# Expert weights in 2 MB transfers, a ring of eleven double slots, and first loads inside the output projection

## What is computed

```python
# x1: the input plus the gated output of the mixer, y_conv and y_ssd (1024 x 1024 each)
x  = x + g1 * (concat([y_conv, y_ssd]) @ w_out)            # w_out 2048 x 2048
h  = modulate(rms_norm(x, norm2_w), sh2, sc2)
s  = sigmoid(h @ w_router)                                 # 32 experts in 8 groups of 4
best = argmax over groups of (sum of the top 2 of s + bias)
idx, gw = top 2 experts inside that group; gw normalised
y  = sum over the two experts e of gw * ((silu(h @ w_gate[e]) * (h @ w_up[e])) @ w_down[e])
out = rms_norm(x + g2 * y, final_norm_w)
```

## Time and profile before

| | |
|---|---|
| median of 3 runs | 2704.45 us |
| the profiled execution | 2700.38 us |
| its span | 2698.6 us |
| TensorE matmul, busy share | 94% |
| VectorE, ScalarE, GpSimd, busy share | 49%, 24%, 11% |
| moved by DMA | 710.43 MB, mean 263 GB/s |
| weights of the experts | 128 + 128 transfers of 1 MB, 64 of 2 MB, each some 31 us from issue to landing |

### The profile page before, as it was taken

One profiled execution on the slowest core, in us unless ns is written; L12 is line 12 of the kernel. 1 busy time (PEld: TensorE's weight loads), 2 busy tenths in 40 slices (PEclk: granted clock), 3 DMA queues, 4 the chain that ended last, 5 costly groups with the idle time before them and its releaser, 6 DMA issues.

```text
span 2698.6 us, 31563 instructions
## 1 busy us (share of the span) xinstructions
PE 2526.9 (94%) x11968; PEld 1517.0 (56%) x11968; DVE 1317.0 (49%) x1583; ACT 641.1 (24%) x897; POOL 295.4 (11%) x505
## 2 busy tenths in 40 slices
PE   4999999999999978999999699899999999999996
PEld 3577888888768866788887333233333333333332
DVE  4369999999785768544336522122222212121224
ACT  4122222222222286322333011011111111011113
POOL 0000000000021111010001111111111111111110
PEclk9999999999999989999999799999999999999998
DMA  9843333333586562755645999999993999999698
GB/s 336 309 130 101 101 109 101 98 109 97 152 287 209 190 218 90 285 170 153 227 132 210 421 414 409 405 362 415 406 407 114 392 403 370 408 406 408 224 412 340
DMA packets 234071, 710.43 MB, mean 263 GB/s; under 512 B 26292, under 2 KB 120644, under 8 KB 186382
## 3 DMA queue, kind: packets, MB, share of 16 engines
q1 hardware_dynamic: 186626, 555.56, 53.4%
q0 software_dynamic: 37344, 125.76, 14.9%
q10 hardware_dynamic: 9998, 27.71, 2.8%
HBM read 657.60 MB, written 69.81 MB: 270 GB/s over the span
## 4 chain that ended last, share of the span: by engine, by line
PE 33%; DMA 23%; DVE 2%; issue 0%; ACT 0%; SPq 0%; POOL 0%; ACTq 0%; DVEq 0%; POOLq 0%
DMA ring<-in_w_down_dram 19%; PE ps L1750 12%; PE ps L1764 7%; PE ps L1979 4%; PE ps L1981 4%; PE ps L1980 4%; DMA ring<-in_w_up_dram 2%; DMA ring<-x_d 1%; PE ps L1773 1%; PE ps L1690 0%; DVE tmp L2256 0%; PE ps L1994 0%; DMA x_d<-orow,oixc 0%; DVE ring L2670 0%; PE ps L1782 0%
## 5 line engine op out<-in xcount | busy, mean ns | idle before, releaser
L1750 PE MATMUL ps<-ring,xT 128*64 128x512 f32 x3136 | 693.0, 599 | 26.4 <-DMA ring<-in_w_up_dram 24.7
L1750 PEld LDWEIGHTS ps<-ring,xT 128*64 128x64 f32 x3136 | 228.8, 138 | 481.8 <-issue 477.4
L1764 PE MATMUL ps<-ring,hidT 128*64 128x512 f32 x1568 | 350.3, 597 | 11.9 <-DVE hidT L2649 5.2
L764 PE MATMUL ps<-hh,wih 128*128 128x512 f32 x1056 | 330.5, 394 | 7.0 <-DVE wil L752 7.0
L2644 DVE TENSOR_TENSOR hb<-ps,gsl 128x256 f32<-128x256 f32 x49 | 20.8, 425 | 646.0 <-ACT gsl L2207 646.0
L764 PE MATMUL ps<-hh,wil 128*128 128x512 f32 x1056 | 331.0, 394 | 0.0
L764 PE MATMUL ps<-hl,wih 128*128 128x512 f32 x1056 | 329.5, 393 | 0.0
L1136 DVE SCALAR_TENSOR_TENSOR acc<-u,vcur,acc 128x1024 f32<-128x1024 f32 x240 | 308.2, 1284 | 7.8
L1764 PEld LDWEIGHTS ps<-ring,hidT 128*64 128x64 f32 x1568 | 107.8, 137 | 220.7 <-issue 192.3
L764 PEld LDWEIGHTS ps<-hh,wih 128*128 128x128 f32 x1056 | 198.8, 189 | 55.2 <-DVE wil L752 7.8
L764 PEld LDWEIGHTS ps<-hl,wih 128*128 128x128 f32 x1056 | 199.1, 189 | 44.4
(11 more groups left out here) (434 smaller groups left out, 3074.4 us busy)
## 6 DMA issues: line engine op xcount, KB each, us to landing
ring<-in_w_gate_dram SPq DMA_DIRECT2D x128, 1024.0 KB, 31.4
ring<-in_w_up_dram SPq DMA_DIRECT2D x128, 1024.0 KB, 31.6
ring<-in_w_down_dram SPq DMA_DIRECT2D x64, 2048.0 KB, 31.8
wm<-in_w_mod_dram POOLq DMA_DIRECT2D x88, 512.0 KB, 4.2
wraw_i<-in_w_in_dram SPq DMA_DIRECT2D x72, 512.0 KB, 3.9
wraw_o<-in_w_out_dram SPq DMA_DIRECT2D x128, 256.0 KB, 3.5
wmA<-in_w_mod_dram SPq DMA_DIRECT2D x32, 512.0 KB, 8.2
u<-in_w_mod_dram POOLq DMA_DIRECT2D x24, 512.0 KB, 4.7
```

What stands on the lines that cost most here:

```text
L764: last = pe.matmul(ps[:, 1024 * r + 512 * h:1024 * r + 512 * h + 512], w[:, s, k, :], x_[:, t, 512 * h:512 * h + 512], start=(t == 0 and n ...
L1750: last = pe.matmul(ps[BLK * a:BLK * a + BLK, BANK_GU:BANK_GU + FE], xT[:, t, h, :], ring[:, s:s + 2, c0:c0 + FE // 2], start=(q + k == 0), ...
L1764: last = pe.matmul(ps[BLK * a:BLK * a + BLK, BANK_D + 512 * n:BANK_D + 512 * n + 512], hidT[:, t, h, :], ring[:, slot(o, 8 + d), c0:c0 + 512],
```

## The change

It has three parts, made together.

1. The ring has eleven double slots of 2 MB (`PAIRS`), all transfers of weights are 2 MB with 16 KB runs, six for an expert (`NP = 6`): gate and up of the first half of the row tiles, gate and up of the second, and two of down. `gate_up` goes in two halves and signals after each. The two operands of a matmul, gate and up, now lie in two double slots whose distance varies, and where the order of the slots would put up first, the two loads are swapped.
2. `ys` and `yc` are laid out by row tile first, so that memory comes free in order during the last column block. The first expert's first two loads are issued in the loop of the projection (at HALF + 56 and HALF + 60, when pieces HALF + 52 and HALF + 56 are used), two more right after it, when HALF + 60 and all pieces are used. For that the order of visits has to be known earlier, and all routing work of the first half of the tokens, with its transposes, moves up by 6 to 20 pieces, and SyncE stores and reads the order inside the loop. Tables get new addresses.
3. The rows of the second half of the tokens are stored in columns 0 to 1023 (at HALF + 35 to 42), 1024 to 1535 (at HALF + 50 to 57), and 1536 to 2047 as before.

```diff
-            NSLOT = 22
-            NP = 8 + FT
-            SLOT = [4, 5, 6, 7, 12, 13, 14, 15, 20, 21, 16, 17, 18, 19, 0, 1, 2, 3, 10, 11, 8, 9]
+            NP = 6
+            PAIRS = [2, 3, 6, 7, 10, 9, 8, 1, 0, 5, 4]
+            NPAIR = len(PAIRS)
+            NSLOT = 2 * NPAIR
+            home, kinds, before_it = {}, {}, {}
+            holder = {}
+            for n in range(NP * E):
+                o, m = n // NP, n % NP
+                if m < 4:
+                    two = [PAIRS[(n - m % 2 + i) % NPAIR] for i in range(2)]
+                    kinds[o, m] = m if two[0] < two[1] else m ^ 1
+                else:
+                    kinds[o, m] = m
+                pair = PAIRS[n % NPAIR]
+                home[o, kinds[o, m]] = pair
+                before_it[o, m] = holder.get(pair)
+                holder[pair] = (o, kinds[o, m])
...
-                if m < 8:
-                    half, t0 = k_tile(q, 0)
-                    src = we_gu[kind][e, half, :, t0:t0 + 4, :].rearrange("a c t f -> (a c) (t f)")
-                    sp.dma_start(ring[:, s, :], src).then_inc(s_we[m], 16)
+                if what < 4:
+                    src = we_gu[what % 2][e, what // 2, :, :, :].rearrange("a c t f -> (a c) (t f)")
...
 # gate_up on TensorE
-                    for q in range(4):
-                        if q % 2 == 0:
-                            pe.wait_ge(s_xT, 2 * j + q // 2 + 1)
+                    for h in range(2):
+                        gate, up = home[o, 2 * h + GATE], home[o, 2 * h + UP]
                         for kind in (GATE, UP):
-                            pe.wait_ge(s_we[2 * q + kind], 16 * o + 16)
...
+                            pe.wait_ge(s_we[2 * h + kind], 16 * o + 16)
+                        for t in range(KT // 2):
+                            if h == 0 and t % 4 == 0:
+                                pe.wait_ge(s_xT, 2 * j + t // 4 + 1)
...
-                        last.then_inc(s_guq[q], 1)
+                        last.then_inc(s_guq[h], 1)
...
 # SyncE, in the loop over the pieces g and behind it
+                        if g == HALF + 50:
+                            sp.wait_ge(s_tab, 1)
+                            sp.dma_start(order_d[:, :], order_w[0:1, :]).then_inc(s_its, 16)
+                        if g == HALF + 52:
+                            sp.wait_ge(s_its, 16)
+                            first_expert = visit(sp, 0)
+                        for m in range(2):
+                            if g == HALF + 56 + 4 * m:
+                                sp.wait_ge(s_wou, HALF + 52 + 4 * m)
+                                load(sp, 0, m, first_expert)
...
-                    sp.wait_ge(s_wou, PIECES)
-                    for m in range(8):
-                        load(sp, 0, m, experts[0])
+                    for m in range(2, 4):
+                        sp.wait_ge(s_wou, HALF + 52 + 4 * m)
+                        load(sp, 0, m, first_expert)
+                    experts = [first_expert, visit(sp, 1)]
                     sp.wait_ge(s_res, 8 * HT)
-                    load(sp, 0, 8, experts[0])
+                    load(sp, 0, 4, experts[0])
                     sp.wait_ge(s_lg, 3 * HT)
-                    load(sp, 0, 10, experts[0])
-                    for m in range(2):
-                        load(sp, 1, m, experts[1])
+                    load(sp, 0, 5, experts[0])
+                    load(sp, 1, 0, experts[1])
...
-                    for m in range(2, 6):
+                    for m in range(1, 3):
                         load(sp, 1, m, experts[1])
+                    sp.wait_ge(s_g2, 1)
+                    load(sp, 1, 3, experts[1])
                     sp.wait_ge(s_tbl, 1)
-                    sp.wait_ge(s_g2, 1)
-                    for m in range(6, 9):
-                        load(sp, 1, m, experts[1])
+                    load(sp, 1, 4, experts[1])
...
+                    for r in range(NPAIR, NP * E):
                         o, m = r // NP, r % NP
...
+                        released(*before_it[o, m])
+                        load(sp, o, m, expert)
...
 # GpSimd, stores of the rows
+                    for c, (c0, c1) in enumerate(((0, 1024), (1024, 1536))):
+                        for j in range(HT, TT):
+                            pool.wait_ge(s_res, 16 + 4 + 4 * c + j - HT + 1)
+                            pool.wait_ge(s_wou, HALF + 35 + 15 * c + j - HT)
+                            pool.dma_start(h2_d[j * P:(j + 1) * P, c0:c1], x1_tile(j)[:, c0:c1]).then_inc(s_h2s[j], 16)
+                        for j in range(HT, TT):
+                            pool.wait_ge(s_wou, HALF + 39 + 15 * c + j - HT)
+                            pool.dma_start(x1_d[j * P:(j + 1) * P, c0:c1], x1_tile(j)[:, c0:c1]).then_inc(s_x1[j], 16)
```

More of the change, by code:

```diff
@@ L1504, in lcols @@
                 return 3584 + E * j + 128 * part
-            s_we = [sem(f"expert_piece_loaded{m}") for m in range(8 + FT)]
+            NP = 6
+            s_we = [sem(f"expert_piece_loaded{m}") for m in range(NP)]
             we_gu = [w.rearrange("e (h c t) f -> e h c t f", h=2, t=KT // 2) for w in (w_gate, w_up)]
@@ L1551, in hybrid_layer @@
             ring = place("ring", [P, NSLOT, D], F32, 0)
-            LAST_FREE = NP * (E - 1) - (NSLOT - NP)
-            free_slot = [SLOT[(LAST_FREE + n) % NSLOT] for n in range(NSLOT - NP)]
-            frow, pjunk, prow = ring[:, free_slot[8], :], ring[:, free_slot[9], :], ring[:, slot(E - 1, 0), :]
+            free_slot = [2 * home[E - 2, m] + i for m in range(NP) if holder[home[E - 2, m]][0] == E - 2 for i in range(2)]
+            assert len(free_slot) == NSLOT - 2 * NP
+            frow, pjunk, prow = ring[:, free_slot[8], :], ring[:, free_slot[9], :], ring[:, 2 * home[E - 1, 0], :]
             same = place("same", [P, 2 * TT, NI], F32, 64 * KB)
[L1556 to L1563, removed]
+            at_visit, before = place("at_visit", [P, E, E], F32, 68 * KB + 256), place("before", [P, E, E], F32, 76 * KB)
+            val = place("val", [P, 2 * TT, NI], F32, 72 * KB + 256)
+            val2 = place("val2", [P, 2 * TT, 2, NI], F32, 68 * KB + 256)
+            hot0 = place("hot0", [P, TT, BLK], F32, 76 * KB + 512)
+            assert 4 * TT * NI * 4 <= 8 * KB + 256
+            i128 = place("i128", [P, P], I32, 82 * KB)
+            ip = place("ip", [P, 1], I32, 83 * KB)
+            iid = place("iid", [P, TT], I32, 83 * KB + 256)
+            pairs = place("pairs", [P, E, E], F32, 84 * KB)
+            gp = place("gp", [P, D], F32, 88 * KB)
             place_at[0] = NSLOT * 8 * KB
@@ L1584, in hybrid_layer @@
             xT_at = place_at[0]
+            hots = [hot0, place("hot1", [P, TT, BLK], F32, xT_at)]
             xT = place("xT", [P, KT // 2, 2, BLK])
-            orow, orow2 = place("orow", [P, HALF_ROW]), ring[:, slot(E - 1, 1), 0:HALF_ROW]
+            orow, orow2 = place("orow", [P, HALF_ROW]), ring[:, 2 * home[E - 1, 0] + 1, 0:HALF_ROW]
             gsl, hb = place("gsl", [P, FE // 2]), place("hb", [P, FE // 2])
@@ L1641, in hybrid_layer @@
             s_fr, s_xf = sem("final_w_loaded"), [sem(f"x1_reloaded{j}") for j in range(TT)]
-            s_guq = [sem(f"gate_up_quarter_done{q}") for q in range(4)]
+            s_guq = [sem(f"gate_up_half_done{q}") for q in range(2)]
             s_dt = [sem(f"down_part_done{t}") for t in range(FT)]
```

154 lines of the change are left out of this document (64 added, 90 removed).

## The result

The kernel after the change takes 2708.29 us (median of 20 runs, from 2702.31), the kernel before 2704.56 us beside it (20 runs, 2701.32 to 2707.66). The ratio is 1.0015 with a 95% interval of 1.0008 to 1.0022, so the change costs 2 to 6 us. One of the 20 runs took 3264.72 us, at a granted clock of 0.745, and is outside the ratio; the other 19 have a median of 2707.91. Two further sets of 12 runs gave 2706.19 and 2706.92 (ratio 1.0009 each): over the three sets the medians stand 3.7, 1.3 and 2.8 us above the kernel before, on average 2.6. The profiled execution took 2703.88 us, its span 2702.0.

What follows compares the result with a forecast made beforehand. TensorE (94% busy) and the DMA engines were taken as nearly level, with stalls where the ring drains empty. Gains from early loads and 16 KB runs against coarser steps summed to +7.1 us: 2704.45 becomes 2711.5, range 2704 to 2718.

Steps and rivals of the forecast that it cites:

- early start: First weight loads issued in the last projection pieces: the 24th MB lands at 1538.1, 3.7 us earlier, not 15.
- 16 KB runs: Gate and up transfers with 16 KB instead of 8 KB runs: 1.3% saved of a DMA-bound stretch, bounds 1% and 2.6%.
- the late restart: A full ring restarts after half, not a quarter, of the last block's gate and up: 3.46 us later, four times.
- the late last wait: After the last wait for gate and up, 6.87 us of matmuls are left, not 3.46, partly at a lower clock.
- B: Stall ended by the fourth quarter's gate and up, block end 1884.27, 6.3 us late before; forecast 5.5 us longer.
- D: Stall ended by a down transfer near 2202.66, 4.8 us late before; forecast 3.5 us longer, 0.8 of it clock.
- E: Stall ended by a down transfer near 2342.47, 4.6 us late before; forecast 3.5 us longer.
- the tail: Last expert's weights and the reload of the rows, one DMA run from 2531 on: forecast 2.0 us longer.
- Rival 3: Nearly nothing: restart hidden because the ring is not quite full, B and E lose 3.46 less; 2704.5, chance 0.10.
- A: Stall whose last down piece starts at 1739.10, 16.2 us late before; forecast -4.8 us, including 0.9 lost to the clock.
- rival 4: Slower: both halves after a long wait run partly at the low clock, four stalls, +10.2 us, 2722; chance 0.13.
- rival 5: Projection disturbed by 2 MB loads before w_out pieces or by lumped vector work: +5 us, 2716.5; chance 0.05.

Runs made afterwards that it cites:

- e6: Kernel after with its early routing, split stores and early first loads, but ring, 1 MB pieces and quarters of the kernel before: 2700.44 us, ratio 0.9986.
- e10: The kernel of e6 run again, unaltered, in another set: 2699.68 us, ratio 0.9978 against the kernel before.
- e2: Kernel after with each 2 MB gate or up load cut into two 1 MB transfers of 8 KB runs: 2710.42 us, ratio 1.0025.
- e11: The kernel of e2 run again, in another set: 2711.63 us, ratio 1.0024 against the kernel before.
- e3: Kernel before, with a gate or up slot free only when its half, not its quarter, is done: 2707.36 us, ratio 1.0010.
- e4: Kernel before, with TensorE starting a half of gate and up only when all four pieces have landed: 2714.95 us, ratio 1.0048.
- e7: Kernel before with the edits of e3 and e4 together: 2715.79 us, ratio 1.0040.
- e1: Kernel after, with the first four weight loads issued only when all projection pieces are done: 2710.84 us, ratio 1.0025.
- e12: Kernel after, unaltered, run again as the measure of its set: 2706.92 us, ratio 1.0009 against the kernel before.
- e5: Kernel after, unaltered, run again as the measure of its set: 2706.19 us, ratio 1.0009 against the kernel before.
- e8: Kernel after, with the rows of the second half of the tokens stored as in the kernel before: 2708.36 us, ratio 1.0007.
- e9: The kernel of e10 with the first half's gate and up in 2 MB transfers of 16 KB runs, quarters for the second: 2700.99 us, ratio 0.9984.

## Why the prediction was right, and which of its terms were not

The forecast was 2711.5, the time 2708.29: slower, by about half of what was forecast (+3.7 against +7.1, and +2.6 over three sets), and within the range of 2704 to 2718. By the prediction's own line of 0.2% (5.4 us) it counts as the same and not as slower. The sum had three kinds of terms. From the medians over the sets, with the stalls that go set against the coarser steps:

```
                              forecast   measured   from
early start, stores              -3.7       -4.4    e6 and e10 against before
16 KB runs                       -8.2       -4.2    three sets of the change against e2 and e11
coarser steps                   +19.0      +11.2    e2 and e11 against e6 and e10
  of it the late restart        +13.8       +3.0    e3 alone
  of it the late last wait       +5.2      +10.6    e4 alone
sum                              +7.1       +2.6
```

The two lines "of it" were each measured alone and add up to 13.6, the line above them to 11.2; e7, both steps on the kernel before, gives 10.9 by another way.

**Early start: right.** The second issue of the entry at 1518.00 landed 8.4 us after 1529.7, at 1538.1. That this is the forecast moment to the tenth is luck: it was issued 1.1 us earlier and took 1.1 us longer than in the forecast. TensorE lost nothing in the projection: its first matmuls behind it start at 1470.73, before at 1471.11. It is worth about 4 us and not the 15 that three free transfers look like, because the ring holds 22 MB either way; e1, with 3 to 4 us, excludes the 15.

**16 KB runs: the rate right, its worth too high.** 1.1% more weights in a full stretch is near the forecast 1.3%, but only half of the 8.2 us shows in the time (e2 stands 2.1 us above the change, e11, in one set with it, 4.7). The lower rate takes 8.2 to some 7; of where the rest goes I have no run, and the uncertainty of the difference, some 2 us, is a part of it. The fixed cost for each transfer stays out: the change merges four pairs an expert, 128 in all, and about 4 us over them is 0.03 us each. The Trainium skill (DMA: Bandwidth & Descriptors, on the anatomy of one DMA) gives about 2.0 us fixed, for transfers that GpSimd issues, and holds most of it to be latency of completion. The weights here are issued by SyncE, and with an expert's transfers queued behind each other no run here shows that latency in the time.

**The late restart: the step that failed.** The prediction put "B: +3.46 (restart)", and the same in D, E and the tail. SyncE's restart did come 3.46 us later, but idle DMA time is not lost time when other work falls into it. From 1763.4, the start of the block, the kernel after moved:

```profile
1763.40:1765.90 2.50, 2.50 (x14) 0.84 (x12) 1.28 (x1) 0.53 (x1) 0.48 (x3) 1.00 0.00 0
1765.90:1768.40 2.50, 2.50 (x16) 0.79 (x14) 0.00 (x0) 0.00 (x0) 2.27 (x4) 1.00 0.33 26
1768.40:1770.90 2.50, 2.50 (x14) 0.81 (x12) 0.00 (x0) 0.00 (x0) 0.71 (x1) 1.00 0.91 159
1770.90:1773.40 2.50, 2.50 (x14) 0.86 (x12) 0.00 (x0) 0.00 (x0) 0.00 (x0) 1.00 1.12 365
1773.40:1775.90 2.50, 2.50 (x14) 0.86 (x12) 0.00 (x0) 0.00 (x0) 0.00 (x0) 1.00 1.00 426
1775.90:1778.40 2.50, 2.50 (x16) 1.36 (x12) 0.42 (x1) 0.38 (x1) 0.00 (x0) 1.00 0.98 419
1778.40:1780.90 2.50, 2.35 (x13) 0.84 (x13) 2.43 (x6) 2.09 (x2) 0.00 (x0) 1.00 0.99 426
```

In these 17.5 us it is 1821 x 2.5 us = 4.55 MB, against 1833 x 2.5 = 4.58 in the seven rows of the kernel before under e3, with 0.90 MB of rows in both: level, with the 16 KB runs in it. So B lost 2.0 us and not 5.5, and the tail 0.6 and not 2.0. Rival 3 had this effect, a hidden restart, but for another reason (a ring not quite full).

**The late last wait: mis-sized the other way.** I had the 4 MB of down behind the last half arrive in a third of an expert's 34.4 us, 11.4 us. In the kernel before the same 4 MB came in D between 2192.91 and 2202.66, in 9.75 (in A 9.73, in E 9.78): the average of a stretch with gathers in it was taken for a stretch without. That is 1.65 us more, three times, which alone takes the 5.2 of the table to 10.2, near the 10.6 of e4. The clock I had at 0.8 in D. There a half took 10.04 us instead of 6.87, at a granted clock of 0.86 in its stretch; at E it took 7.09, at B 8.78 (forecast 8.6), at A 7.09 after the last wait. A's two slow halves (8.57 and 9.16) ran in front of further waits and cost nothing. So rival 4 had the mechanism, and its sign, a clock below 0.9, was seen in A and D (0.86), but not its price. The last halves of the four stalls that are hit change from one execution of the same kernel to the next: B and D here, E alone in e12, none in e5 (TensorE in order of time, E in e12, then D in e5):

```profile
2336.73 8.79 PE L1755 MATMUL ps<-ring,xT 128*64 128x512 f32 x32 [3.67 <-DMA ring<-in_w_up_dram]
```

```profile
2195.20 7.09 PE L1755 MATMUL ps<-ring,xT 128*64 128x512 f32 x32 [2.21 <-DMA ring<-in_w_gate_dram]
```

In A the last half landed at 1724.96, where my terms gave 1739.10 - 11.4 - 6.3 = 1721.4. Of these 3.5 us 1.65 are the 4 MB; the other 1.9 no row explains, and the 16 KB term, 2.6 us there, is the nearest. The 0.9 for the clock was not spent there, which leaves the step 2.9 short.

**Parts without a price: right as far as can be told.** The stores make no difference that shows (e8). The earlier routing and the transfers in front of w_out pieces have no run of their own; together with the early start they gain 4.4 us (e6, e10), and the first block started at 1522.57, under the 1523 that was the sign of rival 5. In other executions it starts near 1526.5, but e3, with this stage as before, has 1525.55.

That the forecast came as near as it did is luck: two errors in the price of coarse steps, 10.8 us too much for the restart and 5.4 too little for the last wait, stood against each other, and the runs had been given 4 us too much gain. The decomposition is good to about 2 us a line; what is sure of it is the order (e4 over e3, e10 under e12) and the gain of e6 and e10 over both kernels.

## What to carry to other kernels

Merging transfers changes two events at once, when a slot is given back and when its data may be used; try each alone, and keep the piece small that ends a stall, since all work behind its landing is exposed, while earlier pieces may be large at little cost (e9). Before a pause of the DMA engines is priced at its length, look at what other transfers run in or right behind it. The best version here keeps the early start and drops the merging (2699.68 us); e9, which merges only the first half, can't be told from it.

## What the runs showed of the hardware

TensorE's granted clock after a wait for weights: of the eleven waits of over 1 us before a half from the stall A on of the kernel after, the five of 1.53 to 2.62 us were followed by halves of 7.09 us, and those of 3.18, 3.56 (twice), 4.60 and 5.35 by halves of 8.57 to 10.04, with stretches granted 0.86 to 0.93, that is, with a part at the lower of the two levels of 1.2 and 2.4 GHz. One of 3.68 us was followed by 7.09. Other executions widen the band: a wait of 1.99 us in e8 was followed by a half of 8.78 us, its start at a granted clock of 0.57, one of 2.26 in e12 by 8.69, and one of 3.69 in e5 by 7.09. The first, and the stretch behind it:

```profile
2327.87 8.78 PE L1755 MATMUL ps<-ring,xT 128*64 128x512 f32 x32 [1.99 <-DMA ring<-in_w_gate_dram]
```

```profile
2328.00:2332.00 4.00, 4.00 (x12) 1.22 (x13) 0.00 (x0) 0.00 (x0) 3.10 (x5) 0.57 1.05 446
```

In quarters it is as mixed: 3.14 us, then 5.35 in e10; 3.16, then 3.65 in the kernel before, but 2.50, then 5.12 there in A. From 2.0 to 3.7 us the same wait may cost nothing or 2 to 3 us.

Indirect transfers of rows keep the engines busy far beyond their bytes: in the stretch at 1768.40 the share is 0.91 at 159 GB/s, where at 1773.40, with the weights running, 426 are reached at 1.00.
